# GpSimd forms the high and low part of the third weight unit at the start of FFN 1, 2 and 3

## The chip, the cores and the metric

The kernel runs on one core of a Trainium2 chip. The core has TensorE (PE in the profile: matmuls; PEld is its weight load), VectorE (DVE), ScalarE (ACT), GpSimd (POOL) and SyncE (SP, which here only issues DMAs). The metric is the device time of one execution in microseconds.

## What is computed

Two layers of a diffusion backbone over 256 latent and 256 context tokens of width 1024. A layer is a half-step SwiGLU FFN, a mixer (differential attention, windowed attention with a sink, and a bidirectional state-space scan, then an output projection) and a second half-step FFN. Each sub-layer is preceded by an RMS norm with shift, scale and gate per stream. Cut to what the change touches:

```python
def swiglu(h, w13, w2):
    g, u = jnp.split(h @ w13, 2, axis=-1)
    return (jax.nn.silu(g) * u) @ w2
...
    xl = xl + 0.5 * ml[2] * swiglu(modulate(rms_norm(xl, norm_ffn1[l]), ml[0], ml[1]), ffn1_w13[l], ffn1_w2[l])
    xc = xc + 0.5 * mc[2] * swiglu(modulate(rms_norm(xc, norm_ffn1[l]), mc[0], mc[1]), ffn1_w13[l], ffn1_w2[l])
```

## The kernel before

**Weights.** Activations lie with the feature on the partitions: `h_hi` and `h_lo`, eight k tiles of 128 x 512 tokens (256 in FFN 3, where only latent tokens are left). Weights come in units of 128 x 2048 float32 (1 MB). Each operand is split into a high part, rounded to fp32r, and a low part, the rest; a product is three matmuls, high by high, high by low, low by high (`mm3`, L1544 to L1546). A unit is loaded by SP into `raw` (slots 0 and 1) or `raw2` (slot 2); its high part is an ACT copy to `w_hi` (`split` of ACT, L553), its low part a DVE subtraction to `w_lo` (`split` of DVE, L942). Slot is the unit's number modulo three.

**The four FFNs** (f = 0 to 3; each layer has two). An FFN has 33 units: first pair of gate and up, then turns i = 1 to 9 of gate, down and up, and a last turn. The units of the first three are: unit 0 (gate, slot 0), unit 1 (up, slot 1), and unit 2 (the gate of turn 1, slot 2, from `raw2`), which is the third unit of the title. PE runs unit 0 in `first_unit` on an input that is scaled but not yet normed, while the norm is computed; unit 1 in `two_tiles(1, ...)`, k by k as the normalised tiles come (it waits for `h_lo_s` before each k); then, in turn 1, it waits for `silu_done` and runs unit 2, then down with slot 0 of the next units.

**The norm chain.** For each of eight tiles DVE multiplies `n_t = x_res * n_rstd` (L1044), ACT applies scale and shift and rounds to `h_hi` (L604, L611), DVE subtracts to `h_lo` (L1047). `n_t` has two buffers, so DVE's step for tile d waits for `h_lo` of tile d - 2. In the middle DVE scales the result of unit 0 in PSUM (`first_scaled`, L1030, L1034). After the chain ACT makes the split of unit 2, loads the table of silu and makes `sg` of unit 0 (`silu_first`, L634); DVE makes the low part of unit 2. Then both go on with `ffn_phase`: split of unit 3 (slot 0), product `gu` and its split to `a_hi` and `a_lo`, split of unit 4 (slot 1).

**Semaphores.** `hi_ready` and `lo_ready` count the high and low parts of all units in order, `unit_done` the units that PE has finished, `raw_in[slot]` the loads. `base` is the number of an FFN's first unit.

**GpSimd** issues loads of the modulation weights (`load_piece`, into `mod_raw`, read by DVE at L965) and, in a mixer, fills some tiles and issues small DMAs (`mixer_rows`). It computes nothing else. Its order is: for each f the loads of that FFN, and after FFN 0 and 2 the mixer's rows.

Of the kernel before, what the change touches and what calls it, by code (L numbers as in the profile page):

```python
# [109 lines left out]
def backbone(nc, x_in, c_in, const_in, cols_in, mod_in, scale_in, ffn_in, proj_in, dt_in, out_w_in, out):  # L110
    with ExitStack() as ctx:
# [124 lines left out]
        def ffn_base(f):  # L236

            return (f // 2) * LAYER_UNITS + (f % 2) * (FFN_UNITS + MIX_UNITS)
# [221 lines left out]
        @block.gpsimd  # L460
        def _(pool):
            def load_piece(q):
                for half in range(2):
                    if not (isinstance(q, int) and q == 0):

                        pool.wait_ge(mod_step, 8 * q + 4 * half - 4)
                    pool.dma_start(mod_raw[:, half], mod_in[2 * q + half]).then_inc(mod_in_s[half], 16)  # L467

            def scale_of(j):
                return scale_w[:, j % 4, :] if j % 4 < 2 else (sg, gu)[j % 2][:, :, :].rearrange("p s t -> p (s t)")  # L470

            def load_scale(j):
                if j >= 4:
                    pool.wait_ge(scale_mm, j - 3)
                pool.dma_start(scale_of(j), scale_in[j]).then_inc(scale_in_s[j % 4], 16)

            def load_half(q, half):
                if q:
                    pool.wait_ge(mod_step, 8 * q + 4 * half - 4)
                pool.dma_start(mod_raw[:, half], mod_in[2 * q + half]).then_inc(mod_in_s[half], 16)  # L480

            def load_stretches(f):
                for lo, hi, q0 in STRETCH[f]:
                    if (f, lo) == (0, 1):
                        with pool.Fori(0, 2) as t:
                            for q in range(3):
                                load_piece(3 * t + (q0 + q))
                    elif q0 is not None:
                        with pool.Fori(lo, hi) as i:
                            load_piece(i + (q0 - lo))  # L490
                if f in LAST_PIECE:
                    load_piece(LAST_PIECE[f])

            def mixer_rows(layer):
                nt = out_tokens(layer)

                pool.wait_ge(spilled, 16 * (layer + 1))
                for r in (e_rows, x_rows):
                    pool.memset(r[:, :].bitcast(F32), 0.0).then_inc(rows_zero, 1)
                pool.wait_ge(h_lo_s, 8 * (3 * layer + 2))  # L500
                pool.memset(rows[0:48, 3, :], 0.0).then_inc(rows_zero, 1)
                if layer == 0:
                    pool.memset(st[:, 2:4, :], 0.0).then_inc(st_zero, 1)
                pool.wait_ge(row_act, ROW_ACTS * (layer + 1))
                pool.dma_start(tot_dram[layer], lam[0:16, 72:76]).then_inc(tot_out, 16)
                pool.wait_ge(cv_ready, 6 * (layer + 1))
                for g in range(2):
                    for d in range(2):
                        pool.dma_start(c_two[64 * d:64 * d + 64, g, 0:nt], cv[64 * g:64 * g + 64, 5, 0:nt]).then_inc(c_two_in, 16)

                pool.wait_ge(tot_out, 16 * (layer + 1))
                for d in range(2):
                    src = tot_dram[layer, 8 * d:8 * d + 8].rearrange("h c -> (h c)")
                    pool.dma_start(etb[64 * d:64 * d + 64].rearrange("p h c -> p (h c)"),
                                   src.partition_broadcast(64)).then_inc(etb_in, 16)

            load_half(0, 0)
            load_scale(0)
            load_scale(1)
            load_half(0, 1)  # L520
            load_scale(2)
            load_scale(3)
            load_half(1, 0)
            load_scale(4)
            load_scale(5)
            load_half(1, 1)
            load_scale(6)
            load_scale(7)
            for f in range(4):
                if f == 1:  # L530

                    pool.wait_ge(mix_lo_s, 8)
                if f in MOD_PRE:
                    for q in range(MOD_PRE[f][0], sum(MOD_PRE[f])):
                        load_piece(q)
                load_stretches(f)
                if f % 2 == 0:
                    mixer_rows(f // 2)
# [3 lines left out]
        def _(act):  # L542
# [19 lines left out]
            def split_next(layer, m):  # L562

                if m < MIX_UNITS:
                    split_mix(layer, m)
                else:
                    split(m - MIX_UNITS, 2 * layer + 1, 0)
# [52 lines left out]
            def silu_gate(f, i, nt):  # L620
                for m in range(2):
                    if not (f == 0 and isinstance(i, int) and i == 0):
                        act.wait_ge(mul_done, 2 * (f * PAIRS + i) - 1 + m)
                    act.activation(sg[:, m, 0:nt], ps[:, m, 0:nt], ACT.Silu).then_inc(silu_done, 1)  # L624
# [17 lines left out]
            def ffn_phase(f):  # L642
                nt, base = ffn_tokens(f), ffn_base(f)
                act.wait_ge(unit_done, base + 1)
                if f == 0:
                    silu_gate(f, 0, nt)
                split(0, f, 1)
                act.wait_ge(unit_done, base + 2)
                round_product(f, 0, nt, a_hi)
                split(1, f, 1)  # L650

                def after_last(m):

                    if f % 2 == 0:
                        split_mix(f // 2, m)
                    elif f < 3:
                        split(m, f + 1, 0)

                def turn(i):
                    act.wait_ge(unit_done, base + 3 * i)  # L660
                    silu_gate(f, i, nt)
                    split(2, f, i)
                    act.wait_ge(unit_done, base + 3 * i + 1)
                    split(0, f, i + 1)
                    act.wait_ge(unit_done, base + 3 * i + 2)
                    round_product(f, i, nt, a_hi)
                    split(1, f, i + 1)

                def last_turn():
                    act.wait_ge(unit_done, base + 3 * LAST)  # L670
                    silu_gate(f, LAST, nt)
                    split(2, f, LAST)
                    act.wait_ge(unit_done, base + 3 * LAST + 1)
                    round_product(f, LAST, nt, b_hi)
                    after_last(0)

                for lo, hi, _ in STRETCH[f]:
                    with act.Fori(lo, hi) as i:
                        turn(i)
                last_turn()  # L680
                if f < 3:
                    n, ntn = NORM_AFTER[f]
                    for d in range(KT):
                        norm_square(n, d, ntn, (y_evac, updated(f, LAST_DOWN, d)))
                        scaled_high(n, d, ntn, h_hi)
                    after_last(1)
                    if f == 1:
                        norm_rest(n, ntn, base + FFN_UNITS)
                        after_last(2)
                        silu_first(f + 1, ffn_tokens(f + 1))  # L690
                    else:
                        norm_root(n, ntn)

            def mixer(layer):
# [50 lines left out]
                    if d in (1, 4, 6):  # L745
                        split_next(layer, MIX_UNITS - 1 + (1, 4, 6).index(d))
                norm_rest(n, nt)
                split_next(layer, MIX_UNITS + 2)
                silu_first(2 * layer + 1, nt)
                if layer == 0:  # L750
                    act.wait_ge(cb_in_s, 32)
# [184 lines left out]
        def _(dve):  # L936
# [141 lines left out]
            def ffn_phase(f):  # L1078
# [7 lines left out]
                        split(m, f + 1, 0)  # L1086

                q0, cnt = MOD_PRE.get(f, (0, 0))
                split(0, f, 1)
                dve.wait_ge(unit_done, base + 2)  # L1090
                product(f, 0, nt, a_hi, a_lo)
# [66 lines left out]
                if f < 3:  # L1158
                    nn, ntn = NORM_AFTER[f]
                    down(LAST_DOWN, base + FFN_UNITS, add_n=(nn, ntn))  # L1160
                    add_square(nn, KT - 1, ntn)
                    for d in (KT - 2, KT - 1):
                        scaled_low(nn, d, ntn, h_hi, h_lo)
                    after_last(1)
                    if f == 1:
                        norm_rest(nn, ntn, {5: lambda: first_scaled(nn, ntn, base + FFN_UNITS)})
                        after_last(2)
                    else:
                        clear_pads()
                else:  # L1170
                    down(LAST_DOWN, base + FFN_UNITS)

            def mixer(layer):
# [57 lines left out]
                        split_next(layer, MIX_UNITS)  # L1231
                split_next(layer, MIX_UNITS + 1)
                norm_rest(n + 1, nt, {5: lambda: first_scaled(n + 1, nt, base + MIX_UNITS)})
                split_next(layer, MIX_UNITS + 2)

            def layer_vectors(layer):
                lv = cols[:, layer, C_LAM:C_LAM + 128]
# [791 lines left out]
```

## Time and profile before

| | us |
|---|---|
| median of 3 runs | 1876.06 (1874.19 to 1877.59) |
| the profiled execution, its time | 1876.09 |
| the profiled execution, its span | 1874.4 |

The mean granted clock of TensorE was 0.975 of full speed. Busy shares of the span: PE 96%, DVE 76%, ACT 40%, POOL 3%. The chain that ended last is 87% PE. The start of FFN 1 lies at about 700 to 750 us, that of FFN 2 at 1060 to 1115, that of FFN 3 at 1655 to 1705. A timeline row gives the start in us, the duration, the engine, the line and the operation with its tiles; brackets at its end give how long the engine stood idle before it and what released it. In the rows of this profile `raw2` is written `raw`.

### The profile page before, as it was taken

Reading aid. Unit: us, or ns where it says so; the run is one execution under the profiler, and the core shown is the slowest. Engines: PE = TensorE matmul, PEld = TensorE weight load, DVE = VectorE, ACT = ScalarE, POOL = GpSimd, SP = SyncE. Lnnn points to the kernel's source line nnn. Section 1 sums busy time; section 2 is a strip of 40 time slices with the busy share of each in tenths; the row PEclk is TensorE's granted clock in tenths of the full one; section 3 lists DMA queues with packets and bytes.
Section 4 is the critical chain, followed back from the end, with each engine's and each line's share of the span. In section 5 each row is a group of like instructions: output and inputs, shape, how many; then the busy total and the mean of one; then the engine's idle time right before and its main releaser. Section 6 shows DMA issues by size and latency. Waiting matters only on the chain.

```text
span 1874.4 us, 26133 instructions
## 1 busy us (share of the span) xinstructions
PE 1805.3 (96%) x9314; PEld 1486.6 (79%) x9314; DVE 1422.5 (76%) x2351; ACT 752.6 (40%) x1147; POOL 51.9 (3%) x101
## 2 busy tenths in 40 slices
PE   8999999998998899999999999999999799899999
PEld 5788888886776577888888878888888587589999
DVE  5899977888787766877778668787876888666665
ACT  4322222246555657222222462222225665564342
POOL 1000000000000000000000000000000000000000
PEclk8999999999999899999999999999999899799999
DMA  8445544513312032444444324444332223034543
GB/s 350 177 178 205 198 157 157 197 51 120 124 46 91 1 135 90 157 159 161 173 157 156 113 93 177 157 151 180 139 136 83 75 74 142 16 113 180 186 175 110
DMA packets 37588, 259.50 MB, mean 138 GB/s; under 512 B 4369, under 2 KB 5841, under 8 KB 7441
## 3 DMA queue, kind: packets, MB, share of 16 engines
q1 hardware_dynamic: 26066, 182.32, 26.6%
q0 software_dynamic: 11456, 76.32, 11.2%
q8 instruction: 39, 0.64, 0.1%
q14 instruction: 27, 0.22, 0.0%
HBM read 252.60 MB, written 5.24 MB: 138 GB/s over the span
## 4 chain that ended last, share of the span: by engine, by line
PE 87%; ACT 6%; DVE 4%; issue 2%; DMA 1%; POOL 0%; ACTq 0%; DVEq 0%; POOLq 0%
PE ps L1544 25%; PE ps L1545 25%; PE ps L1546 25%; PE ps L1648 2%; ACT n_t L604 1%; PE ps L1855 1%; PE ps L1820 1%; PE ps L1797 1%; ACT h_hi L611 1%; DMA scale_w<-scale_in 1%; PE ps L1830 1%; ACT w_hi L553 1%; PE ps L1916 1%; PE ps L1580 1%; PE ps L1584 1%
## 5 line engine op out<-in xcount | busy, mean ns | idle before, releaser
L1544 PE MATMUL ps<-h_hi,w_hi 128*128 128x512 f32 (+1 forms) x1792 | 662.4, 370 | 33.0 <-DVE w_lo L947 17.6
L1545 PE MATMUL ps<-h_lo,w_hi 128*128 128x512 f32 (+1 forms) x1792 | 654.8, 365 | 0.0
L1546 PE MATMUL ps<-h_hi,w_lo 128*128 128x512 f32 (+1 forms) x1792 | 653.9, 365 | 0.0
L1544 PEld LDWEIGHTS ps<-h_hi,w_hi 128*128 128x128 f32 x1792 | 341.1, 190 | 97.7 <-DVE w_lo L947 19.2
L1546 PEld LDWEIGHTS ps<-h_hi,w_lo 128*128 128x128 f32 x1792 | 341.1, 190 | 55.3
L1545 PEld LDWEIGHTS ps<-h_lo,w_hi 128*128 128x128 f32 x1792 | 341.4, 191 | 53.9 <-issue 1.0
L942 DVE TENSOR_TENSOR w_lo<-raw,w_hi 128x2048 fp32r<-128x2048 f32 x132 | 301.9, 2287 | 87.1 <-ACT w_hi L553 87.0
L553 ACT ACTIVATE w_hi<-raw 128x2048 fp32r<-128x2048 f32 x132 | 252.3, 1911 | 256.1 <-PE ps L1546 256.1
L1070 DVE SCALAR_TENSOR_TENSOR x_res<-ps,abg,x_res 128x256 f32<-128x256 f32 x584 | 248.5, 477 | 139.7 <-PE ps L1546 138.6
L965 DVE CUSTOM_DVE_ANT_0 mod_prod<-mod_raw,cb 128x1024 f32<-128x1024 f32 x256 | 301.3, 1218 | 0.2 <-DVE mod_t L969 0.2
L1544 PE MATMUL ps<-a_hi,w_hi 128*128 128x512 f32 (+1 forms) x640 | 233.2, 364 | 4.5 <-DVE x_res L1070 4.5
L1545 PE MATMUL ps<-a_lo,w_hi 128*128 128x512 f32 (+1 forms) x640 | 232.9, 364 | 0.0
L1546 PE MATMUL ps<-a_hi,w_lo 128*128 128x512 f32 (+1 forms) x640 | 232.9, 364 | 0.0
L640 ACT ACTIVATE a_hi<-gu 128x512 fp32r<-128x512 f32 (+1 forms) x80 | 44.2, 579 | 317.5 <-DVE gu L1061 317.5
L1544 PEld LDWEIGHTS ps<-a_hi,w_hi 128*128 128x128 f32 x640 | 121.5, 190 | 24.0 <-DVE x_res L1070 5.1
L1546 PEld LDWEIGHTS ps<-a_hi,w_lo 128*128 128x128 f32 x640 | 121.4, 190 | 18.9
L1545 PEld LDWEIGHTS ps<-a_lo,w_hi 128*128 128x128 f32 x640 | 121.4, 190 | 18.9
L624 ACT ACTIVATE sg<-ps 128x512 f32<-128x512 f32 (+1 forms) x82 | 40.3, 544 | 225.8 <-PE ps L1546 225.8
L1061 DVE TENSOR_TENSOR gu<-ps,sg 128x512 f32<-128x512 f32 (+1 forms) x88 | 50.8, 619 | 51.1 <-PE ps L1546 50.8
L947 DVE TENSOR_TENSOR w_lo<-raw,w_hi 128x2048 fp32r<-128x2048 f32 (+1 forms) x30 | 64.4, 2154 | 14.4 <-ACT w_hi L560 14.2
L467 POOL DMA_DIRECT2D mod_raw<-mod_in x64 | 33.8, 529 | 1190.9 <-DVE mod_acc L965 988.2
L604 ACT ACTIVATE n_t<-n_t,abg 128x256 f32<-128x256 f32 x88 | 48.1, 590 | 22.2 <-DVE n_t L1467 12.6
(237 smaller groups left out, 1672.9 us busy)
## 6 DMA issues: line engine op xcount, KB each, us to landing
raw<-ffn_in SPq DMA_DIRECT2D x132, 1024.0 KB, 4.8
mod_raw<-mod_in POOLq DMA_DIRECT2D x68, 1024.0 KB, 5.0
raw<-proj_in SPq DMA_DIRECT2D x20, 1024.0 KB, 4.8
raw<-out_w_in SPq DMA_DIRECT2D x8, 1024.0 KB, 5.1
x_spill<-x_res SPq DMA_DIRECT2D x2, 2048.0 KB, 7.8
x_res<-x_spill SPq DMA_DIRECT2D x2, 2048.0 KB, 8.3
scale_w<-scale_in POOLq DMA_DIRECT2D x4, 512.0 KB, 12.8
x_res<-x_in SPq DMA_DIRECT2D x2, 1024.0 KB, 10.8
```

Of the source, the lines that this page charges most:

```text
L553: act.activation(w_hi[:, slot, :], raw_of(slot), ACT.Copy).then_inc(hi_ready, 1)
L604: act.activation(seg, seg, ACT.Identity, scale=abg[:, n, 0, s, d:d + 1], bias=abg[:, n, 1, s, d:d + 1]).then_inc(aff_done, 1)
L624: act.activation(sg[:, m, 0:nt], ps[:, m, 0:nt], ACT.Silu).then_inc(silu_done, 1)
L640: act.activation(dst[:, m, 0:nt], gu[:, m, 0:nt], ACT.Copy).then_inc(act_hi_s, 1)
L942: tt(w_lo[:, slot, :], raw_of(slot), w_hi[:, slot, :], ALU.subtract).then_inc(lo_ready, 1)
L947: tt(w_lo[:, m % 3, 0:n], raw[:, m % 2, 0:n], w_hi[:, m % 3, 0:n], ALU.subtract).then_inc(lo_ready, 1)
L965: dve.tensor_tensor_reduce(mod_prod[:, s], mod_raw[:, j // 2, j % 2], cb[:, s, :], 1.0, 0.0, ALU.mult, ALU.add, mod_acc[:, s, j:j + 1]).th ...
L1061: tt(gu[:, m, 0:nt], ps[:, 2 + m, 0:nt], sg[:, m, 0:nt], ALU.mult).then_inc(mul_done, 1)
L1070: last = stt(out=seg, in0=ps[:, bank, s * LAT:(s + 1) * LAT], scalar=abg[:, n, 2, s, d:d + 1], in1=seg, op0=ALU.mult, op1=ALU.add)
L1544: pe.matmul(dst, w_hi[:, slot, wsl], hi, start=first, stop=False)
L1545: pe.matmul(dst, w_hi[:, slot, wsl], lo, start=False, stop=False)
L1546: return pe.matmul(dst, w_lo[:, slot, wsl], hi, start=False, stop=last)
```

## The change

The split of the third unit of FFN 1, 2 and 3 is taken from ACT (three copies) and DVE (three subtractions), where it stood behind the norm chain. GpSimd does both parts: `split_third(f)` waits for the load, for PE to have left slot 2, and for the low part of the unit before it (`lo_ready`, base + 2), copies to `w_hi`, waits for that, and subtracts to `w_lo`. In GpSimd's program it stands ahead of the modulation loads of that FFN. ACT and DVE get a wait for its counts ahead of their split of slot 0, so that the counters stay in order. FFN 0 and the splits of the mixers are untouched.

```diff
--- before.py
+++ after.py
@@ -514,6 +514,16 @@
                     pool.dma_start(etb[64 * d:64 * d + 64].rearrange("p h c -> p (h c)"),
                                    src.partition_broadcast(64)).then_inc(etb_in, 16)
 
+            def split_third(f):
+
+                base = ffn_base(f)
+                pool.wait_ge(raw_in[2], 16 * f * PAIRS + 16)
+                pool.wait_ge(unit_done, base)
+                pool.wait_ge(lo_ready, base + 2)
+                pool.tensor_copy(w_hi[:, 2, :], raw2[:, :]).then_inc(hi_ready, 1)
+                pool.wait_ge(hi_ready, base + 3)
+                pool.tensor_tensor(w_lo[:, 2, :], raw2[:, :], w_hi[:, 2, :], ALU.subtract).then_inc(lo_ready, 1)
+
             load_half(0, 0)
             load_scale(0)
             load_scale(1)
@@ -530,6 +540,8 @@
                 if f == 1:
 
                     pool.wait_ge(mix_lo_s, 8)
+                if f > 0:
+                    split_third(f)
                 if f in MOD_PRE:
                     for q in range(MOD_PRE[f][0], sum(MOD_PRE[f])):
                         load_piece(q)
@@ -644,6 +656,8 @@
                 act.wait_ge(unit_done, base + 1)
                 if f == 0:
                     silu_gate(f, 0, nt)
+                else:
+                    act.wait_ge(hi_ready, base + 3)
                 split(0, f, 1)
                 act.wait_ge(unit_done, base + 2)
                 round_product(f, 0, nt, a_hi)
@@ -686,7 +700,6 @@
                     after_last(1)
                     if f == 1:
                         norm_rest(n, ntn, base + FFN_UNITS)
-                        after_last(2)
                         silu_first(f + 1, ffn_tokens(f + 1))
                     else:
                         norm_root(n, ntn)
@@ -745,7 +758,6 @@
                     if d in (1, 4, 6):
                         split_next(layer, MIX_UNITS - 1 + (1, 4, 6).index(d))
                 norm_rest(n, nt)
-                split_next(layer, MIX_UNITS + 2)
                 silu_first(2 * layer + 1, nt)
                 if layer == 0:
                     act.wait_ge(cb_in_s, 32)
@@ -1086,6 +1098,8 @@
                         split(m, f + 1, 0)
 
                 q0, cnt = MOD_PRE.get(f, (0, 0))
+                if f > 0:
+                    dve.wait_ge(lo_ready, base + 3)
                 split(0, f, 1)
                 dve.wait_ge(unit_done, base + 2)
                 product(f, 0, nt, a_hi, a_lo)
@@ -1164,7 +1178,6 @@
                     after_last(1)
                     if f == 1:
                         norm_rest(nn, ntn, {5: lambda: first_scaled(nn, ntn, base + FFN_UNITS)})
-                        after_last(2)
                     else:
                         clear_pads()
                 else:
@@ -1231,7 +1244,6 @@
                         split_next(layer, MIX_UNITS)
                 split_next(layer, MIX_UNITS + 1)
                 norm_rest(n + 1, nt, {5: lambda: first_scaled(n + 1, nt, base + MIX_UNITS)})
-                split_next(layer, MIX_UNITS + 2)
 
             def layer_vectors(layer):
                 lv = cols[:, layer, C_LAM:C_LAM + 128]
```

GpSimd, from the end of the first mixer's rows into FFN 1. Before (`load_piece` is L467, its loop L489):

```order
L509 DMA c_two<-cv 64x512 x4
L514 DMA etb<-decay_totals 64x32 x2
L489 UNCONDITIONAL_BRANCH
L489 ISA
L467 ISA
L467 DMA mod_raw<-mod_in 128x2048
```

After:

```order
L509 DMA c_two<-cv 64x512 x4
L514 DMA etb<-decay_totals 64x32 x2
L523 CAST w_hi<-raw2 128x2048
L525 ISA
L525 TENSOR_TENSOR w_lo<-raw2,w_hi 128x2048
L489 UNCONDITIONAL_BRANCH
L489 ISA
```

The copy and the subtraction have come in ahead of the loop of loads.

ACT, from the last tile of the norm chain into FFN 3. Before:

```order
L604 ACTIVATE n_t<-n_t,abg 128x256
L611 ACTIVATE h_hi<-n_t 128x256
L553 ACTIVATE w_hi<-raw2 128x2048
L634 ACT_TABLE_LOAD
L634 ACTIVATE sg<-ps,bias 128x256 x2
L553 ACTIVATE w_hi<-raw 128x2048
```

After (the line numbers are those of the changed kernel, 12 higher here):

```order
L616 ACTIVATE n_t<-n_t,abg 128x256
L623 ACTIVATE h_hi<-n_t 128x256
L646 ACT_TABLE_LOAD
L646 ACTIVATE sg<-ps,bias 128x256 x2
L565 ACTIVATE w_hi<-raw 128x2048
L652 ACTIVATE a_hi<-gu 128x256 x2
```

The copy of `raw2` is gone, and the table load follows the chain at once.

DVE, from the end of the norm chain into FFN 1. Before:

```order
L1044 TENSOR_TENSOR n_t<-x_res,n_rstd 128x512
L1047 TENSOR_TENSOR h_lo<-n_t,h_hi 128x512 x2
L942 TENSOR_TENSOR w_lo<-raw2,w_hi 128x2048
L942 TENSOR_TENSOR w_lo<-raw,w_hi 128x2048
L1061 TENSOR_TENSOR gu<-ps,sg 128x512 x2
```

After:

```order
L1056 TENSOR_TENSOR n_t<-x_res,n_rstd 128x512
L1059 TENSOR_TENSOR h_lo<-n_t,h_hi 128x512 x2
L954 TENSOR_TENSOR w_lo<-raw,w_hi 128x2048
L1073 TENSOR_TENSOR gu<-ps,sg 128x512 x2
L1076 TENSOR_TENSOR a_lo<-gu,a_hi 128x512 x2
```

The subtraction of `raw2` is gone between the last `h_lo` and the low part of slot 0.

## Rows read from the trace of the kernel before

**Rows 1.** The page, part 1: busy us, share of the span, instructions.

```profile
PE 1805.3 (96%) x9314; PEld 1486.6 (79%) x9314; DVE 1422.5 (76%) x2351; ACT 752.6 (40%) x1147; POOL 51.9 (3%) x101
```

**Rows 2.** Waits of PE: engine line <- releaser: us in total, times, longest.

```profile
PE ps L1544 <- DVE h_lo L1047: 4.6, 7, 0.9
PE ps L1544 <- ACT sg L634: 3.0, 2, 1.5
PE ps L1544 <- DVE w_lo L942: 2.7, 1, 2.7
```

**Rows 3.** Timeline of PE at the three starts: start us, us, operation [idle before].

```profile
737.36 0.49 PE L1544 MATMUL ps<-h_hi,w_hi 128*128 128x512 f32 x1 [1.49 <-ACT sg L634]
...
1102.86 0.49 PE L1544 MATMUL ps<-h_hi,w_hi 128*128 128x512 f32 x1 [1.48 <-ACT sg L634]
...
1691.10 0.39 PE L1544 MATMUL ps<-h_hi,w_hi 128*128 128x256 f32 x1 [2.69 <-DVE w_lo L942]
```

**Rows 4.** Timeline of ACT at the start of FFN 1.

```profile
732.43 1.90 ACT L553 ACTIVATE w_hi<-raw 128x2048 fp32r<-128x2048 f32 x1
734.35 1.28 ACT L634 ACT_TABLE_LOAD   x1
735.65 1.57 ACT L634 ACTIVATE sg<-ps,bias 128x256 f32<-128x256 f32 x4
```

**Rows 5.** Timeline of ACT at the start of FFN 3.

```profile
1686.82 1.90 ACT L553 ACTIVATE w_hi<-raw 128x2048 fp32r<-128x2048 f32 x1
1690.03 0.84 ACT L634 ACTIVATE sg<-ps,bias 128x256 f32<-128x256 f32 x2
```

**Rows 6.** Timeline of DVE at the start of FFN 1.

```profile
714.03 2.28 DVE L942 TENSOR_TENSOR w_lo<-raw,w_hi 128x2048 fp32r<-128x2048 f32 x1
717.28 1.29 DVE L1044 TENSOR_TENSOR n_t<-x_res,n_rstd 128x512 f32<-128x512 f32 x2 [0.96 <-ACT n_rstd L596]
719.86 0.69 DVE L1047 TENSOR_TENSOR h_lo<-n_t,h_hi 128x512 fp32r<-128x512 f32 x1 [1.29 <-ACT h_hi L611]
...
732.56 0.69 DVE L1047 TENSOR_TENSOR h_lo<-n_t,h_hi 128x512 fp32r<-128x512 f32 x1 [0.96 <-ACT h_hi L611]
734.37 2.29 DVE L942 TENSOR_TENSOR w_lo<-raw,w_hi 128x2048 fp32r<-128x2048 f32 x1 [1.11 <-ACT w_hi L553]
...
757.10 1.22 DVE L965 CUSTOM_DVE_ANT_0 mod_prod<-mod_raw,cb 128x1024 f32<-128x1024 f32 x1
```

**Rows 7.** Timeline of DVE at the starts of FFN 2 and FFN 3.

```profile
1079.16 2.29 DVE L942 TENSOR_TENSOR w_lo<-raw,w_hi 128x2048 fp32r<-128x2048 f32 x1 [0.32 <-ACT w_hi L553]
1082.78 1.29 DVE L1044 TENSOR_TENSOR n_t<-x_res,n_rstd 128x512 f32<-128x512 f32 x2 [1.32 <-ACT n_rstd L596]
1085.36 0.69 DVE L1047 TENSOR_TENSOR h_lo<-n_t,h_hi 128x512 fp32r<-128x512 f32 x1 [1.28 <-ACT h_hi L611]
...
1674.81 2.28 DVE L942 TENSOR_TENSOR w_lo<-raw,w_hi 128x2048 fp32r<-128x2048 f32 x1
1677.61 0.76 DVE L1044 TENSOR_TENSOR n_t<-x_res,n_rstd 128x256 f32<-128x256 f32 x2 [0.52 <-ACT n_rstd L596]
1679.20 0.42 DVE L1047 TENSOR_TENSOR h_lo<-n_t,h_hi 128x256 fp32r<-128x256 f32 x1 [0.84 <-ACT h_hi L611]
...
1688.75 2.29 DVE L942 TENSOR_TENSOR w_lo<-raw,w_hi 128x2048 fp32r<-128x2048 f32 x1 [1.38 <-ACT w_hi L553]
```

**Rows 8.** Busy time by windows, FFN 3: window, length, busy by engine, PEclk, DMA share, GB/s.

```profile
1692.00:1696.00 4.00, 4.00 (x23) 4.00 (x22) 3.09 (x4) 1.25 (x3) 0.00 (x0) 0.57 0.72 262
```

**Rows 9.** Timeline of POOL and of DVE beside it, mixer of layer 0.

```profile
428.13 0.53 POOL L499 MEMSET e_rows<- 128x512 f32 x1 [45.48 <-DMA x_spill<-x_res]
...
444.71 0.95 POOL L503 MEMSET st<- 128x1024 f32 x1
...
444.34 3.11 DVE L1261 SCALAR_TENSOR_TENSOR cv<-xpad,cols,cv 128x512 f32<-128x512 f32 x4
...
1466.97 3.11 DVE L1261 SCALAR_TENSOR_TENSOR cv<-xpad,cols,cv 128x512 f32<-128x512 f32 x4
```

## The prediction

> **What bounds the kernel now.** I read the page's first part, then the waits of TensorE (PE), then the timelines of the four engines where an FFN begins. PE is busy for 96% of the span [rows 1], and inside the FFN turns it hardly waits. So a split that leaves ScalarE (ACT) or VectorE (DVE) in a full turn is worth nothing; what counts is the start of an FFN. There PE works through unit 0, then unit 1, one k at a time, as the normalised tiles h_lo arrive, then needs two things for the third unit: sg of unit 0 (ACT, L634), and w_lo of slot 2 (DVE, L942). The reader is to see three waits. At the starts of FFN 1 and FFN 2 PE idles 1.49 and 1.48 us for sg; at FFN 3 it idles 2.69 us for w_lo [rows 2, 3]. Just ahead of each, ACT makes w_hi of the third unit in 1.90 us, then loads a table (1.28), then makes sg [rows 4, 5]. On DVE the third w_lo comes last, behind the whole norm chain [rows 6, 7]. The PE wait for h_lo, 4.6 us over seven places [rows 2], says that the norm chain on DVE and ACT is itself close to PE's heels.
>
> **What the change takes away.** Three ACT copies (1.90 each) and three DVE subtractions (2.29 each) leave the row between the norm chain and sg. FFN 1: ACT's sg ended at 735.65 + 1.57 = 737.22 and PE went on at 737.36; 1.90 earlier is 735.32, when PE is still in unit 1, so the whole idle time goes: 1.49. FFN 2 has the same shape: 1.48. FFN 3: sg ended at 1690.03 + 0.84 = 1690.87, w_lo at 1688.75 + 2.29 = 1691.04, PE went on at 1691.10. Without the copy sg ends at 1688.97 and PE goes on at about 1689.1: 2.0. What is late next there is sg itself. The sum is **-5.0 us**, if GpSimd (POOL) has w_lo ready and disturbs nobody.
>
> **Is POOL in time?** It may begin when DVE has the low part of slot 1: 714.03 + 2.28 = 716.3, 1079.16 + 2.29 = 1081.5, 1674.81 + 2.28 = 1677.1 [rows 6, 7]. PE wants the result at 735.9, 1101.4 and 1689.1. So the pair of instructions has 19.6, 19.9 and 12.0 us. No row shows POOL reading a tensor. Its fills of 128x512 and 128x1024 took 0.53 and 0.95 us [rows 9], 0.42 us per 512 elements, so one stream of 2048 is 0.53 + 3 x 0.42 = 1.8 us. For the copy I take 1.9 (ACT's copy is 1.90 [rows 4]); its bounds are 1.8 and twice that. The subtraction reads two streams: the bounds are 1.8 (all streams at once) and 4.6 (twice DVE's 2.29); I take two streams, 3.5. Together 5.4, at most some 8.4, inside 12.0. In time.
>
> **What the waits add.** DVE now waits for POOL's low part ahead of its split of slot 0, ACT for POOL's high part; behind these are queued that split, the product and every update of turn 1. Both arrive there at 737 or later at FFN 1, POOL is done by 725: nothing. It would cost from the moment that POOL is later than the table above. On POOL the split stands ahead of the loads of the modulation pieces: at FFN 1 two loads move from before the norm chain to behind the split, about 723 to 725, and DVE first reads them at 757.10 [rows 6]: over 30 us of cover. At FFN 2 it is the same pair. SP's order is unchanged, and its next load of raw2 is released earlier. Nothing here costs.
>
> **The new overlap, and here I choose.** The pair runs exactly in the norm chain, whose DVE steps n_t (x_res, n_rstd) and h_lo (n_t, h_hi) read two SBUF tensors each. The rows bound the disturbance from below: a fill of 128x1024 on POOL, 444.71 to 445.66, lay inside four DVE instructions with two SBUF inputs that took 3.11, as they did with POOL idle [rows 9]. But a fill reads nothing. From above the bound is that either engine reads at a time. Then, at FFN 1: the copy holds 716.35 to 718.25, n_t starts there and not at 717.28 (1.0 late), the pair of n_t ends at 719.55, the subtraction gets the gap and holds until 723.05, and the first h_lo starts there and not at 719.86: the chain is 3.2 late. ACT, which needs about as long per tile as DVE's two steps and the waits between, can't catch up, so sg is late by that too. FFN 2: copy until 1083.4 against n_t at 1082.78; subtraction 1084.7 to 1088.2 against h_lo at 1085.36: 2.8. FFN 3: copy until 1679.05 against 1677.61; subtraction 1679.8 to 1683.3 against 1679.20: 4.1. PE goes on, against before, by -1.9 + 3.2 = +1.3, -1.9 + 2.8 = +0.9 and -2.0 + 4.1 = +2.1: **+4.3 us**. With the subtraction at 1.8 or 4.6 this is -0.8 or +7.6; with the copy twice as long, 5.7 more.
> I take the upper case, since only the operation that reads could show the sharing and the fills can't speak for it. The Trainium skill, "SBUF — State Buffer", section "Summary: rules for kernel authors", says the same of a DVE operation with two SBUF inputs beside a GpSimd operation that reads SBUF: the one that comes second is blocked until the first is finished. No row here shows it; by it the sum is +4.3, without it -5.0. "GPSIMD Engine Reference", section 3.1, gives 4497 ns for the fp32 subtraction's kin (an add of 2048 elements); by that the sum would be some +7.3.
>
> **The clock.** After the 2.69 us of idle PE at FFN 3 the granted clock is 0.57 in 1692 to 1696 [rows 8], so for a part of that window the lower of the two levels (1.2 of 2.4 GHz): 0.43 x 4 = 1.7 us lost. After idle times of 1.5 at FFN 1 and 2 no such row stands. If the chain is 3 us late, FFN 1 and 2 idle for 2.4 to 2.8, like FFN 3 before. Bounds: 0, and 1.7 for each of two, plus a longer one at FFN 3; I take one, +1.7.
>
> **The sum:** +4.3 + 1.7 = +6.0 us. The profiled execution took 1876.09 (span 1874.4 and 1.7 around it), the median is 1876.06, so I put it on the median: **1882.1**.
>
> **Rivals.**
> 1. No interference. Speaks for it: the fills beside DVE. -5.0, and the dip of the clock may go too, but DVE's first update at FFN 3 then sets the pace, so little of the 1.7 is gained: 1871. This is the other side. It decides where the chain is under 1.9 us late.
> 2. The two engines share at a finer grain, and DVE slows by part: half of the delays, 1.6, 1.4 and 2.0, gives -0.3, -0.5 and 0.0: 1875.3, no difference.
> 3. POOL's copy, which rounds, is far slower than its fills: at twice 1.9 and with turns taken +4.3 + 5.7 + 1.7 = +11.7: 1887.8. Past 12 us for the pair PE waits for w_lo at FFN 3 directly.
>
> **Chances.** Forecast 0.50, rival one 0.25, rival two 0.17, rival three 0.08. 0.2% (3.8 us) is about what a measurement of this kernel can tell from no change. Of the forecast's own span (-0.8 to +7.6, with 0 to 5 of clock) about a quarter lies within 0.2%. Slower 0.37 + 0.08 = 0.45; same 0.13 + 0.17 + 0.03 = 0.33; faster 0.22. Both signs hold much, so: the forecast's own range is 1876 to 1888; the range for 8 in 10 takes in rival one and ends above the upper sum: 1870.5 to 1889.
>
> **What would show it.** Right: n_t at the three starts longer or later beside POOL's two instructions, the first h_lo 2.8 to 4 us later against the low part of slot 1, PE's wait for h_lo (4.6 before) at 8 or more, and some wait for sg left. Wrong: n_t and h_lo at 0.69 as before, the waits for sg at FFN 1 and 2 gone and 0.8 us of idle left at FFN 3; or a PE or DVE wait on POOL's w_lo, which would mean that POOL is over 12 us.

## The result, and the profile after

| | before | changed |
|---|---|---|
| median, us (8 runs each) | 1875.12 (1871.44 to 1877.59) | 1882.93 (1880.62 to 1886.46) |
| ratio, 95% interval | | 1.0039 (1.0027 to 1.0051) |
| span of the profiled execution | 1874.4 | 1881.4 |

The kernel became 7.8 us slower (forecast +6.0, from 1876.06 to 1882.1). The interval leaves out 1, so this is a real loss of 0.4%. The page's first part, against [rows 1]: POOL has six instructions and 20 us more; DVE is busy 9 us more, although three subtractions left it.

```profile
PE 1807.7 (96%) x9314; PEld 1485.4 (79%) x9314; DVE 1431.8 (76%) x2348; ACT 747.8 (40%) x1144; POOL 72.1 (4%) x107
```

The waits of PE (released by: us in total, times, longest), against [rows 2]. The lines of code are 12 higher in the changed kernel.

```profile
PE ps L1556 <- DVE h_lo L1059: 11.4, 11, 5.7
...
PE ps L1556 <- DVE x_res L1082: 6.1, 2, 4.5
...
PE ps L1556 <- ACT sg L646: 2.0, 3, 0.8
```

The wait for h_lo rose from 4.6 to 11.4 us, half of it in one place of FFN 3. That for sg fell from 3.0 to 2.0, and the wait for w_lo of [rows 2] (2.7) is gone. The wait for x_res is 6.1 in two places; before it was 4.5 in one.

FFN 1 in the changed kernel, timelines of POOL, then DVE, then ACT, against [rows 4, 6]:

```profile
718.34 1.89 POOL L523 CAST w_hi<-raw 128x2048 fp32r<-128x2048 f32 x1 [218.71 <-DVE w_lo L954]
720.32 4.93 POOL L525 TENSOR_TENSOR w_lo<-raw,w_hi 128x2048 fp32r<-128x2048 f32 x1
...
715.89 2.29 DVE L954 TENSOR_TENSOR w_lo<-raw,w_hi 128x2048 fp32r<-128x2048 f32 x1
719.13 6.66 DVE L1056 TENSOR_TENSOR n_t<-x_res,n_rstd 128x512 f32<-128x512 f32 x2 [0.95 <-ACT n_rstd L608]
725.72 0.68 DVE L1059 TENSOR_TENSOR h_lo<-n_t,h_hi 128x512 fp32r<-128x512 f32 x1
...
720.88 1.10 ACT L616 ACTIVATE n_t<-n_t,abg 128x256 f32<-128x256 f32 x2 [1.85 <-DVE n_t L1056]
...
725.89 1.09 ACT L616 ACTIVATE n_t<-n_t,abg 128x256 f32<-128x256 f32 x2 [3.26 <-DVE n_t L1056]
```

The row of n_t is a pair of 128x512 multiplications: 6.66 us where it was 1.29. ACT shows when each of the two was ready. It began tile 0 at 720.88, behind the end of POOL's copy (720.23) and one multiplication, and tile 1 at 725.89, behind the end of the subtraction (725.25) and the other. So POOL's copy held the first, and the subtraction held the second. From then on DVE's steps are at 0.69 again, but nothing is caught up: counted from the start of the low part of slot 1 (715.89, before 714.03), the first h_lo is 4.00 us late and the last 4.31. The last one started at 738.73, before at 732.56 [rows 6].

The same at FFN 2 and FFN 3, DVE, against [rows 7]:

```profile
1083.49 2.29 DVE L954 TENSOR_TENSOR w_lo<-raw,w_hi 128x2048 fp32r<-128x2048 f32 x1 [0.32 <-ACT w_hi L565]
1087.11 6.28 DVE L1056 TENSOR_TENSOR n_t<-x_res,n_rstd 128x512 f32<-128x512 f32 x2 [1.32 <-ACT n_rstd L608]
...
1678.58 2.28 DVE L954 TENSOR_TENSOR w_lo<-raw,w_hi 128x2048 fp32r<-128x2048 f32 x1
1681.38 6.46 DVE L1056 TENSOR_TENSOR n_t<-x_res,n_rstd 128x256 f32<-128x256 f32 x2 [0.51 <-ACT n_rstd L608]
```

PE, against [rows 3]: where it goes on with the third unit in the three FFNs, and two more waits at FFN 3.

```profile
741.72 0.49 PE L1556 MATMUL ps<-h_hi,w_hi 128*128 128x512 f32 x1 [0.60 <-ACT sg L646]
...
1109.31 0.49 PE L1556 MATMUL ps<-h_hi,w_hi 128*128 128x512 f32 x1 [0.60 <-ACT sg L646]
...
1688.32 0.55 PE L1556 MATMUL ps<-h_hi,w_hi 128*128 128x256 f32 x1 [5.70 <-DVE h_lo L1059]
...
1697.90 0.38 PE L1556 MATMUL ps<-h_hi,w_hi 128*128 128x256 f32 x1 [0.81 <-ACT sg L646]
...
1708.40 0.39 PE L1556 MATMUL ps<-a_hi,w_hi 128*128 128x256 f32 x1 [1.61 <-DVE x_res L1082]
```

The unchanged program ahead of FFN 1 ran 1.86 us later in this execution (low part of slot 1 at 715.89, before at 714.03), so I take distances from the start of that instruction to PE's third unit: FFN 1 25.83 against 23.33, FFN 2 (from 1083.49) 25.82 against 23.70, FFN 3 (from 1678.58) 19.32 against 16.29. That is +2.50, +2.12 and +3.03, in all **+7.65 us**, and the medians differ by 7.8. So the loss lies in the three starts. The spans of the two profiled executions differ by 7.0 only, because they drift apart in stretches that the change doesn't touch: from the third unit of FFN 2 to the low part of slot 1 of FFN 3 the changed kernel took 569.27 us, the kernel before 571.95, and the other kernels of this document lie between 568.6 and 571.3.

The windows of FFN 3 (length, busy by engine, PEclk, DMA share, GB/s), against [rows 8]:

```profile
1684.00:1688.00 4.00, 0.00 (x0) 0.00 (x0) 4.00 (x2) 0.41 (x2) 3.56 (x1) 0.71 0.29 123
1688.00:1692.00 4.00, 3.68 (x17) 3.71 (x18) 3.15 (x8) 3.79 (x8) 0.00 (x0) 0.50 0.72 262
```

### The profile page after: what moved, and what is told of

It is laid out like the page before. It is cut to its first block, busy times and chain, and to the rows that moved or that the text cites. A ratio compares the mean times of both kernels' runs of the same rounds, so it can differ in the third digit from the quotient of the medians.

```text
span 1881.4 us, 26142 instructions
## 1 busy us (share of the span) xinstructions
PE 1807.7 (96%) x9314; PEld 1485.4 (79%) x9314; DVE 1431.8 (76%) x2348; ACT 747.8 (40%) x1144; POOL 72.1 (4%) x107
## 4 chain that ended last, share of the span: by engine, by line
PE 86%; ACT 6%; DVE 5%; issue 2%; DMA 1%; POOL 0%; ACTq 0%; DVEq 0%; POOLq 0%
PE ps L1556 25%; PE ps L1557 25%; PE ps L1558 25%; PE ps L1660 2%; ACT n_t L616 1%; DVE n_t L1056 1%; PE ps L1867 1%; PE ps L1832 1%; PE ps L1809 1%; DMA scale_w<-scale_in 1%; ACT h_hi L623 1%; ACT w_hi L565 1%; PE ps L1928 1%; PE ps L1592 1%; PE ps L1596 1%
## 5 line engine op out<-in xcount | busy, mean ns | idle before, releaser
L954 DVE TENSOR_TENSOR w_lo<-raw,w_hi 128x2048 fp32r<-128x2048 f32 x129 | 295.2, 2288 | 88.8 <-ACT w_hi L565 88.7
L565 ACT ACTIVATE w_hi<-raw 128x2048 fp32r<-128x2048 f32 x129 | 246.6, 1912 | 256.8 <-PE ps L1558 256.8
L467 POOL DMA_DIRECT2D mod_raw<-mod_in x64 | 34.0, 531 | 891.6 <-DVE mod_acc L977 871.7
## 6 DMA issues: line engine op xcount, KB each, us to landing
x_res<-x_in SPq DMA_DIRECT2D x2, 1024.0 KB, 11.4
```

What stands on the lines that cost most here:

```text
L565: act.activation(w_hi[:, slot, :], raw_of(slot), ACT.Copy).then_inc(hi_ready, 1)
L954: tt(w_lo[:, slot, :], raw_of(slot), w_hi[:, slot, :], ALU.subtract).then_inc(lo_ready, 1)
```

## Experiments

The theory: a GpSimd instruction that reads SBUF and a DVE instruction with two SBUF inputs exclude each other, each for its whole length. Rivals: the waits and the moved loads cost the time; any GpSimd work holds DVE; the hold is as long as GpSimd has work, not as long as an instruction.

**Take GpSimd's work away, keep everything else.** The low part's subtraction is replaced in the same way.

```diff
-                pool.tensor_copy(w_hi[:, 2, :], raw2[:, :]).then_inc(hi_ready, 1)
+                pool.memset(w_hi[:, 2, 0:1].bitcast(F32), 0.0).then_inc(hi_ready, 1)
```

> The changed kernel, with GpSimd's copy and subtraction replaced by fills of one column (0.1 us each): the third unit of FFN 1, 2 and 3 is left unsplit and PE multiplies with what lay there. Theory (the loss is the overlap of GpSimd's reads with the norm chain, and the gain of taking the work from ACT and DVE is real): n_t pairs at 1.29, 1.29 and 0.76 us again, no wait for sg at FFN 1 and 2, about 0.8 us of idle PE left at FFN 3, and 5.0 us less than the kernel before: 0.997. Rival (the waits that were added, or the moved loads of the modulation pieces, cost time): slower than or equal to the kernel before, since those stay.

Measured 0.9977 (0.9963 to 0.9991) of the kernel before, 1870.89 against 1874.18. Timelines of DVE at FFN 1, of DVE at FFN 3, and of PE at FFN 3:

```profile
716.57 1.29 DVE L1056 TENSOR_TENSOR n_t<-x_res,n_rstd 128x512 f32<-128x512 f32 x2 [0.95 <-ACT n_rstd L608]
...
1667.28 2.29 DVE L954 TENSOR_TENSOR w_lo<-raw,w_hi 128x2048 fp32r<-128x2048 f32 x1
...
1681.67 0.38 PE L1556 MATMUL ps<-h_hi,w_hi 128*128 128x256 f32 x1 [0.80 <-ACT sg L646]
...
1692.16 0.38 PE L1556 MATMUL ps<-a_hi,w_hi 128*128 128x256 f32 x1 [1.61 <-DVE x_res L1082]
```

The pair of n_t takes 1.29 again. The waits for sg at FFN 1 and 2 are gone, at FFN 3 0.80 us of it is left: the distance to PE's third unit is 14.39, 1.90 less than before. 1.49 + 1.48 + 1.90 = 4.9 us of waits is the gain of relieving ACT and DVE, as the prediction had it. The distances to PE's third unit give a little more, 1.66, 1.65 and 1.90 or 5.2 in all; the medians give 3.3, and the interval (1.7 to 6.9 us) holds all three. At FFN 3 DVE's updates set the next pace: at 1692.16 PE waits 1.61 us for one. The rival with the waits and the moved loads falls: they are all in this kernel.

**Let GpSimd write, but not read.** A fill of 128x2048 for the copy, two for the subtraction.

```diff
-                pool.tensor_copy(w_hi[:, 2, :], raw2[:, :]).then_inc(hi_ready, 1)
+                pool.memset(w_hi[:, 2, :].bitcast(F32), 0.0).then_inc(hi_ready, 1)
...
-                pool.tensor_tensor(w_lo[:, 2, :], raw2[:, :], w_hi[:, 2, :], ALU.subtract).then_inc(lo_ready, 1)
+                pool.memset(w_lo[:, 2, :].bitcast(F32), 0.0).then_inc(again, 1)
+                pool.wait_ge(again, f)
+                pool.memset(w_lo[:, 2, :].bitcast(F32), 0.0).then_inc(lo_ready, 1)
```

> The changed kernel, with GpSimd's copy replaced by a fill of 128x2048 and the subtraction by two such fills, 1.8 us each, so about 5.5 us of GpSimd at the same place (the third unit is left unsplit, zeros are multiplied). Theory (only GpSimd's reads hold DVE's two-input instructions): n_t pairs stay at 1.29 and 0.76 us, time like with one-column fills, -5 us. Rival (any GpSimd instruction that is busy in SBUF holds DVE): n_t pairs of 3 to 6 us, the first h_lo 3 to 4 us late, +3 us or more over the kernel before.

Measured 0.9981 (0.9969 to 0.9993). POOL, then DVE, at FFN 1:

```profile
718.00 1.81 POOL L524 MEMSET w_hi<- 128x2048 f32 x1 [218.65 <-DVE w_lo L957]
719.87 1.81 POOL L526 MEMSET w_lo<- 128x2048 f32 x1
721.74 1.81 POOL L528 MEMSET w_lo<- 128x2048 f32 x1
...
718.80 1.29 DVE L1059 TENSOR_TENSOR n_t<-x_res,n_rstd 128x512 f32<-128x512 f32 x2 [0.95 <-ACT n_rstd L611]
721.38 0.69 DVE L1062 TENSOR_TENSOR h_lo<-n_t,h_hi 128x512 fp32r<-128x512 f32 x1 [1.28 <-ACT h_hi L626]
```

5.4 us of fills lie over the pair of n_t and the first h_lo, and these take 1.29 and 0.69 as before. A GpSimd instruction that only writes doesn't hold DVE; the second rival falls.

**Double the subtraction.**

```diff
-                pool.tensor_tensor(w_lo[:, 2, :], raw2[:, :], w_hi[:, 2, :], ALU.subtract).then_inc(lo_ready, 1)
+                pool.tensor_tensor(w_lo[:, 2, :], raw2[:, :], w_hi[:, 2, :], ALU.subtract).then_inc(again, 1)
+                pool.wait_ge(again, f)
+                pool.tensor_tensor(w_lo[:, 2, :], raw2[:, :], w_hi[:, 2, :], ALU.subtract).then_inc(lo_ready, 1)
```

> The changed kernel, with GpSimd's subtraction made twice into the same tile. Theory (each GpSimd instruction that reads holds the next two-input instruction of DVE for its own length, some 4.2 us for the subtraction): the second subtraction holds DVE once more; if it takes the port at once, the chain is 4.2 us later per start, +12 us over the changed kernel, +20 over the kernel before (1.0105). Where DVE's waiting n_t gets in between the two, the delay is the same but falls on a later step. Rival (the delay comes from the wait chain and not from the length of the subtraction): no more than +1 us over the changed kernel. It also asks for the clock: with PE idle for 4 us more at FFN 1 and 2, a fall of the granted clock there would add 1 to 3 us, which the changed kernel did not show there.

Measured 1.0107 (1.0092 to 1.0122), 1894.44 against 1874.56: +19.9, forecast +20. POOL, DVE and PE at FFN 1, then a window there:

```profile
719.82 4.92 POOL L526 TENSOR_TENSOR w_lo<-raw,w_hi 128x2048 fp32r<-128x2048 f32 x1
724.83 4.85 POOL L528 TENSOR_TENSOR w_lo<-raw,w_hi 128x2048 fp32r<-128x2048 f32 x1
...
718.63 6.67 DVE L1059 TENSOR_TENSOR n_t<-x_res,n_rstd 128x512 f32<-128x512 f32 x2 [0.95 <-ACT n_rstd L611]
725.22 5.00 DVE L1062 TENSOR_TENSOR h_lo<-n_t,h_hi 128x512 fp32r<-128x512 f32 x1
...
730.37 0.76 PE L1559 MATMUL ps<-h_hi,w_hi 128*128 128x512 f32 x1 [4.03 <-DVE h_lo L1062]
...
730.00:735.00 5.00, 4.63 (x11) 3.70 (x12) 4.12 (x7) 3.89 (x8) 0.74 (x2) 0.50 0.80 275
```

The second subtraction ended at 729.68, and the first h_lo, which stood waiting from 725.22, took 5.00 instead of 0.69. Each subtraction costs one hold: the distances to PE's third unit (29.83, 29.83 and 23.47) are 4.00, 4.01 and 4.15 us longer than in the changed kernel, together 12.2. The rival, a delay that doesn't depend on the subtraction's length, falls. Here PE stood for 4.03 us at FFN 1, and behind it the granted clock is 0.50, the lower level, for a whole window of 5 us. So the fall that the prediction had put at FFN 1 or 2 comes with this longer stop. It added nothing to the time: the last h_lo is later by the same 4.00, 4.02 and 4.15 us, so the chain and not PE set the pace.

**Only the copy on GpSimd, at the same place.** The subtraction goes back to DVE behind the norm chain. The edit, cut to GpSimd's part (the counters are adapted so that the order of the units stays):

```diff
+                pool.wait_ge(raw_in[2], 16 * f * PAIRS + 16)
+                pool.wait_ge(unit_done, ffn_base(f))
+                pool.wait_ge(lo_ready, ffn_base(f) + 2)
+                pool.tensor_copy(w_hi[:, 2, :], raw2[:, :]).then_inc(third_hi, 1)
```

> Only the copy goes to GpSimd, behind the low part of slot 1 as in the changed kernel; the subtraction stays on DVE behind the norm chain. Theory (an instruction of GpSimd holds DVE for its own length, 1.89 us less the time for which DVE was idle): n_t starts 1.1, 0.6 and 1.5 us late, the chain with it. PE then waits for w_lo, which ends 2.29 us behind the chain and not 1.90 + 2.29: per start -1.5 or less and +1.1, in all about -1 us, within 0.2% of before. Rival (the hold is not per instruction but for as long as both are in the chain): the same 4 us late chain as in the changed kernel.

Measured 0.9993 (0.9978 to 1.0008), no difference, as expected. POOL and DVE at FFN 1, then PE's third unit in the three FFNs:

```profile
715.66 1.90 POOL L522 CAST w_hi<-raw 128x2048 fp32r<-128x2048 f32 x1 [217.02 <-DVE w_lo L952]
...
716.45 2.25 DVE L1054 TENSOR_TENSOR n_t<-x_res,n_rstd 128x512 f32<-128x512 f32 x2 [0.96 <-ACT n_rstd L606]
719.99 0.69 DVE L1057 TENSOR_TENSOR h_lo<-n_t,h_hi 128x512 fp32r<-128x512 f32 x1 [1.28 <-ACT h_hi L621]
...
735.68 0.50 PE L1554 MATMUL ps<-h_hi,w_hi 128*128 128x512 f32 x1 [0.58 <-DVE w_lo L952]
...
1099.93 0.49 PE L1554 MATMUL ps<-h_hi,w_hi 128*128 128x512 f32 x1 [0.26 <-DVE w_lo L952]
...
1686.33 0.39 PE L1554 MATMUL ps<-h_hi,w_hi 128*128 128x256 f32 x1 [1.23 <-DVE w_lo L952]
```

The first h_lo comes 3.54 us behind the start of n_t, before 2.58 [rows 6]: the chain is 0.96 late. That is the copy's 1.90 less the 0.96 in which DVE was idle anyway: the delay is the instruction's length less the time in which DVE wanted nothing. The rival, a chain that is 4 us late, falls. By the distances from the low part of slot 1, which started at 713.21, 1077.46 and 1670.11 (22.47, 22.47, 16.22), PE goes on 0.9, 1.2 and 0.1 us earlier than before, together 2.2; about 1 was expected, and the interval holds both.

**The changed kernel in quarters.** Copy and subtraction each as four instructions of 512 columns; the diff shows the copy, and the subtraction is cut in the same way.

```diff
-                pool.tensor_copy(w_hi[:, 2, :], raw2[:, :]).then_inc(hi_ready, 1)
+                for c in range(4):
+                    x = pool.tensor_copy(w_hi[:, 2, 512 * c:512 * c + 512], raw2[:, 512 * c:512 * c + 512])
+                x.then_inc(hi_ready, 1)
```

> The changed kernel, with GpSimd's copy and subtraction each cut into four of 512 columns. Theory (the hold is per instruction, whoever comes first): a quarter of the copy holds DVE for at most 0.5 us, a quarter of the subtraction for at most 1.1 to 1.3; DVE's steps get in between, so the delays fall on several tiles, and DVE's own idle time (about 0.2 us per tile, more at the start) takes up part: chain 2 to 3.5 us late and not 4.2, the time +1 to +5 over the kernel before, 1 to 4 under the changed kernel. Rival (the hold lasts as long as GpSimd has work queued): as the changed kernel, +7.8. Second rival (quarters cost much more on GpSimd, so that its low part comes after 12 us): a wait of PE for w_lo at FFN 3.

Measured 1.0036 (1.0022 to 1.0049), 1880.41 against 1874.56: +5.9 by the medians. POOL's rows are merged, four instructions in each; then two of DVE's steps, at FFN 1:

```profile
717.28 3.20 POOL L524 CAST w_hi<-raw 128x512 fp32r<-128x512 f32 x4 [218.54 <-DVE w_lo L959]
720.57 6.37 POOL L528 TENSOR_TENSOR w_lo<-raw,w_hi 128x512 fp32r<-128x512 f32 x4
...
720.88 1.53 DVE L1064 TENSOR_TENSOR h_lo<-n_t,h_hi 128x512 fp32r<-128x512 f32 x1 [0.87 <-ACT h_hi L628]
...
724.02 1.77 DVE L1064 TENSOR_TENSOR h_lo<-n_t,h_hi 128x512 fp32r<-128x512 f32 x1
```

The two engines take turns: every DVE step here waits out one quarter of the subtraction and takes 1.5 to 1.8 instead of 0.69, and POOL's four take 6.37. The third rival falls, since a DVE step gets in after each quarter. The chain has almost no idle time of DVE to hide a quarter in (0.23 us per tile), so the sum of the holds counts, however it is cut. The distances (low part of slot 1 at 714.83, 1081.88 and 1677.06, PE's third unit at 740.11, 1107.04 and 1695.61) give +1.95, +1.46 and +2.26, together 5.7 where the changed kernel has 7.65. That is a relief of 2 us, at the low end of the 1 to 4 expected; the two ratios alone (1.0036 and 1.0039) can't tell it from none. The loss lies above the +1 to +5 that was given, since the last h_lo was 3.3 to 4.2 us late and not 2 to 3.5.

**Copy earlier.** As the fourth experiment, without its wait for the low part of slot 1:

```diff
-                pool.wait_ge(lo_ready, ffn_base(f) + 2)
```

> As the one before, but GpSimd copies as soon as PE has left slot 2 and the load has landed, ahead of the low part of slot 1 (about 709 at FFN 1), where DVE has some slack before the norm's mean. Theory: DVE's sums and scaled tiles are held up to 1.9 us there, of which the row of the mean leaves 1.6 free; the norm chain is 0 to 0.6 us late; then -1.5, -1.5 and about -1.0: 3 to 4.5 us less than the kernel before, 0.998. Rival (the hold just moves ahead of the mean): the mean comes up to 1.9 us late, and the time is that of before or above.

Measured 0.9984 (0.9972 to 0.9997), 1870.9 against 1874.18. POOL and DVE at FFN 1, POOL and DVE at FFN 2, DVE at FFN 3, PE at FFN 3, and a window of FFN 3:

```profile
710.88 2.11 POOL L521 CAST w_hi<-raw 128x2048 fp32r<-128x2048 f32 x1 [210.27 <-PE ps L1555]
...
711.34 2.33 DVE L1032 SCALAR_TENSOR_TENSOR u_lo<-x_res,abg,u_hi 128x256 fp32r<-128x256 f32 x2
...
716.75 2.29 DVE L951 TENSOR_TENSOR w_lo<-raw,w_hi 128x2048 fp32r<-128x2048 f32 x1
718.95 1.29 DVE L1053 TENSOR_TENSOR n_t<-x_res,n_rstd 128x512 f32<-128x512 f32 x2
...
1074.94 1.90 POOL L521 CAST w_hi<-raw 128x2048 fp32r<-128x2048 f32 x1 [66.50 <-PE ps L1555]
...
1074.83 0.88 DVE L1079 SCALAR_TENSOR_TENSOR x_res<-ps,abg,x_res 128x256 f32<-128x256 f32 x2 [0.45 <-PE ps L1555]
1075.62 2.55 DVE L1019 TENSOR_TENSOR n_acc<-n_acc,n_t 128x512 f32<-128x512 f32 x2
...
1664.31 1.97 DVE L1019 TENSOR_TENSOR n_acc<-n_acc,n_t 128x256 f32<-128x256 f32 x1 [0.48 <-ACT n_t L591]
...
1685.09 0.39 PE L1553 MATMUL ps<-h_hi,w_hi 128*128 128x256 f32 x1 [1.23 <-DVE w_lo L951]
...
1676.00:1680.00 4.00, 4.00 (x21) 3.78 (x20) 3.36 (x11) 3.49 (x8) 0.00 (x0) 0.57 0.37 156
```

The copy holds a step of u_lo (2.33 for two of 0.88 in all) ahead of the norm's mean, and at FFN 3 a sum (1.97 for 0.42). The pair of n_t follows the low part of slot 1 without a gap, where a gap of 0.96 stood before: that slack paid. Since the low part of slot 1 is itself late here, distances are taken from the low part of slot 0, which started at 703.59 and 1661.14 (before 702.33 and 1666.56). By them the first h_lo is 0.4 us late at FFN 1 and 0.9 at FFN 3, where 0 to 0.6 was expected, and PE's third unit at FFN 3 is 0.6 us earlier, where 1.0 was expected. PE has no wait at FFN 1 and 2, and 1.23 for w_lo at FFN 3.

FFN 2 shows which steps of DVE are held. Its two updates of x_res, whose tiles are one in PSUM and one in SBUF, ran from 1074.83 to 1075.71, the second of them wholly beside the copy, and took 0.88 as in the kernel before. The sums of n_acc right behind them, with both inputs in SBUF, took 2.55; the copy ended 1.13 after the updates. In the kernel before, the same two sums took 1.48:

```profile
1075.78 1.48 DVE L1010 TENSOR_TENSOR n_acc<-n_acc,n_t 128x512 f32<-128x512 f32 x2
```

So beside this copy a DVE step with one SBUF tile wasn't held, and one with two was.

At FFN 3 PE stood 1.68 us for the first h_lo (0.92 before), and behind that the granted clock is 0.57 in 1676 to 1680. The dip fell into unit 1, and at 1681.94 PE was waiting for the next h_lo again (0.29 us).

This version is 3.3 us faster than the kernel before and, by the two ratios, about 10 faster than the changed kernel. It is the best complete kernel of those run, though its interval ends near 1.

## Why the prediction was right

**What bounds the kernel, and what the change takes away: right.** The waits for sg and w_lo at the three starts were worth 4.9 us in the kernel without GpSimd's work (1.49, 1.48, 1.90; forecast 1.49, 1.48, 2.0).

**POOL in time, the added waits, the moved loads: right.** At FFN 1 the pair took 1.89 and 4.93 us and was done at 725.25, with PE wanting it at 741. No wait of PE, ACT or DVE on POOL stands in the trace.

**The overlap: the mechanism right, its size too small.** The prediction chose that either engine reads at a time, and so it was. The copy was put at 1.9 and took 1.89. The mis-sized term is the subtraction, "I take two streams, 3.5". Its rows say 4.93, 4.91 and 4.55; some 4.3 of that held DVE (at FFN 1 from 720.9, when the first n_t was through, to 725.25), and the rest was its own wait. The first h_lo came 4.00, 3.62 and 4.79 us late, together 12.4, where 3.2, 2.8 and 4.1, together 10.1, were forecast: 0.8 us per start, as much as 4.3 is above 3.5. A second detail was wrong: the subtraction came in between the two multiplications of the pair, not behind them. So tile 1 was held directly and reached ACT late: the second h_lo then waited 0.56 us for ACT at FFN 1, where it had waited 0.23 before. By the last h_lo the chain had lost 0.7 us more over the three starts. The three starts cost +7.65 where the overlap's term was +4.3. The prediction's upper bound for the subtraction (4.6, sum +7.6) meets the 7.65, but with a hold that is 0.3 too long.

The Trainium skill gives 4497 ns in "GPSIMD Engine Reference", section 3.1, for an addition of that size. The 4.55 us of FFN 3 are near it.

The Trainium skill, "SBUF — State Buffer", section "Summary: rules for kernel authors", has the second one to issue fully blocked until the first finishes. The traces agree: 5.00 us for a step of 0.69 beside a subtraction, 0.69 beside a fill.

**The clock: wrong.** +1.7 was added for a fall at FFN 1 or 2, on the argument that PE would idle there for 2.4 to 2.8 us. There was no fall in the changed kernel: PE's idle time there came in pieces of 0.8 us and less, and the granted clock is 1.00:

```profile
735.85 0.50 PE L1556 MATMUL ps<-h_hi,w_hi 128*128 128x512 f32 x1 [0.82 <-DVE h_lo L1059]
...
735.00:740.00 5.00, 3.87 (x15) 2.58 (x15) 2.87 (x5) 4.62 (x7) 0.00 (x0) 1.00 0.03 11
```

At FFN 3 PE stood 5.70 us, and the clock is 0.71 and then 0.50 of full speed in 1684 to 1692. PE stood until 1688.32 and then worked at the lower level without a gap, but by 1695.18 it was waiting for the next h_lo again (0.29 us), so the late norm chain and not the clock set the time. Before, the 0.57 fell into the third unit [rows 8], and in the changed kernel that unit runs at 1.00. What this gave back PE lost again waiting 1.61 us for x_res at 1708.40, as rival one had it of DVE's first update: a low part further on in FFN 3 starts 42.01 us behind that of slot 1 (1720.59), before 38.81 (1713.62), so the +3.03 at the third unit had become +3.2. The dip was longer and moved to where it costs nothing.

**Luck in the total.** The overlap was 3.4 too small and the clock 1.7 too large, which leaves the change 1.8 too small (6.0 against 7.8). The forecast stood on the first median, 0.9 above the later one, and that halved what was left. That the time came out within 1 us is partly luck.

**Rivals.** Rival one, no interference, is what only the kernels with fills in place of the reads show (0.9977 and 0.9981). Rival two, half of the delays, did not occur: they were larger than forecast. Rival three fell with the copy, which took 1.89 us against ACT's 1.90.

## What to carry to other kernels

GpSimd was not a free engine beside a DVE chain whose steps read two SBUF tensors: each GpSimd instruction that read SBUF added its own length to that chain, less what DVE would have idled, and cutting it into quarters took only 2 of 7.65 us away. Give it one-input work (a copy costs 1.89 us here, as on ACT) and put it where the DVE chain has slack, not directly ahead of the step that everyone waits for. Price such a move by the distance between two fixed instructions in the trace: executions of one kernel spread over 6 us here (1871.44 to 1877.59), and the effects were 3 to 8.

## What the runs showed of the hardware

- A subtraction of 128x2048 float32 on GpSimd took 4.55 to 4.93 us against DVE's 2.29; the copy to fp32r took 1.89, as ACT's 1.90; a fill of 128x2048 took 1.81. Quarters of 128x512 took 4 x 0.67 to 0.8 for the copy, so about 1 us more in all.
- Reads hold, writes don't: beside three fills, n_t and h_lo kept 1.29 and 0.69 us; beside a copy and a subtraction the pair of n_t took 6.66.
- What is held is a DVE step with two SBUF inputs: beside the early copy at FFN 2 two steps with one input in PSUM kept their 0.88 us, and the two-input sums behind them took 2.55 instead of 1.48. That is one place in one trace, with a copy; beside a subtraction no such step lay.
- The order of arrival decides between single instructions: POOL's waiting subtraction came in between two back-to-back multiplications of DVE, and DVE's waiting step between two quarters of POOL.
- The clock: a fall to the lower level came in or behind PE stops of 4.03 us (FFN 1, doubled subtraction), 5.70 us (FFN 3, changed kernel), 2.69 us (FFN 3, before, with three stops of 0.3 to 0.9 ahead of it) and 1.68 us (FFN 3, early copy). None followed the stop of 1.49 at FFN 1 before, nor the pieces of up to 0.8 there in the changed kernel.
